# Block sums of W_down and of the stored middle tiles formed earlier and kept in device memory, in a fused transformer layer

## What is computed

```python
        hf = rms_norm(x, ffn_norm[l])
        gate_f, up = jnp.split(hf @ w_gate_up[l], 2, axis=-1)
        x = x + (jax.nn.silu(gate_f) * up) @ w_down[l]
```

## Time and profile before

| | us |
|---|---|
| median of 3 runs (1418.54 to 1420.36) | 1419.81 |
| the profiled execution | 1418.84 |
| its span on the core | 1416.9 |
| TensorE busy | 1297.3 (92%) |
| VectorE busy | 828.2 (58%) |
| ScalarE busy | 458.7 (32%) |
| GpSimd busy | 387.6 (27%) |

### The profile page before, as it was taken

The page is one execution under the profiler, slowest core; times in us unless marked ns, Lnnn a source line. Parts: engine busy times, 40 slices in busy tenths (PEclk is TensorE's granted clock), DMA queues, the critical chain, the costliest instruction groups (busy, mean ns, idle before and its releaser), DMA issues.

```text
span 1416.9 us, 16898 instructions
## 1 busy us (share of the span) xinstructions
PE 1297.3 (92%) x6028; PEld 1024.0 (72%) x6028; DVE 828.2 (58%) x1290; ACT 458.7 (32%) x758; POOL 387.6 (27%) x347
## 2 busy tenths in 40 slices
PE   4999999998898898999969999999999976898888
PEld 3688778886787777644448888888888855676777
DVE  5346778546455565313445555555555567887974
ACT  4221333341233322222343333333333333342421
POOL 3001101330121121100542333222333335564631
PEclk7899999998899999999979999999999998999999
DMA  6311334535521130031312222222224252414132
GB/s 205 107 46 30 107 87 132 169 134 139 182 71 57 45 91 9 0 132 61 104 30 90 87 69 84 74 90 90 90 89 157 67 187 74 134 45 145 36 99 85
DMA packets 155026, 132.00 MB, mean 93 GB/s; under 512 B 16638, under 2 KB 130636, under 8 KB 154956
## 3 DMA queue, kind: packets, MB, share of 16 engines
q1 hardware_dynamic: 154832, 131.03, 29.8%
q10 hardware_dynamic: 124, 0.04, 0.0%
HBM read 93.30 MB, written 36.70 MB: 92 GB/s over the span
## 4 chain that ended last, share of the span: by engine, by line
PE 71%; DVE 14%; issue 7%; ACT 4%; POOL 2%; DMA 2%; ACTq 0%; SPq 0%; DVEq 0%; POOLq 0%; PEldq 0%
PE ps L2028 28%; PE ps L1696 11%; PE ps L2033 9%; PE ps L1944 8%; PE ps L1820 5%; PE ps L1893 3%; DVE wop_lo L1597 2%; DVE dop_lo L1603 2%; DVE x L1658 2%; PE ps L1921 2%; PE ps L1909 1%; DMA w_pair<-hidden 1%; DVE stage L1346 1%; DVE row_stat L1549 1%; POOL mla_sc L777 1%
## 5 line engine op out<-in xcount | busy, mean ns | idle before, releaser
L2028 PE MATMUL ps<-xop_hi,wop_hi 128*128 128x512 f32 x616 | 242.3, 393 | 18.6 <-DVE wop_lo L1597 7.0
L2028 PE MATMUL ps<-xop_lo,wop_hi 128*128 128x512 f32 x616 | 241.6, 392 | 0.0
L2028 PE MATMUL ps<-xop_hi,wop_lo 128*128 128x512 f32 x616 | 241.4, 392 | 0.0
L2033 PE MATMUL ps<-dop_hi,wop_hi 128*128 128x512 f32 x308 | 126.9, 412 | 40.9 <-DVE x L1658 40.8
L1597 DVE TENSOR_TENSOR wop_lo<-w_sumS,wop_hi 128x512 fp32r<-128x512 f32 (+2 forms) x152 | 117.4, 773 | 79.5 <-ACT wop_hi L1117 79.5
L2028 PEld LDWEIGHTS ps<-xop_hi,wop_hi 128*128 128x128 f32 x616 | 116.8, 190 | 45.3 <-DVE wop_lo L1597 14.9
L2028 PEld LDWEIGHTS ps<-xop_hi,wop_lo 128*128 128x128 f32 x616 | 116.8, 190 | 24.5
L2028 PEld LDWEIGHTS ps<-xop_lo,wop_hi 128*128 128x128 f32 x616 | 116.8, 190 | 24.0
L856 POOL TENSOR_TENSOR w_sumS<-w_pair 128x512 f32<-128x512 f32 (+2 forms) x38 | 49.2, 1294 | 308.1 <-DVE wop_lo L1597 275.9
L1597 DVE TENSOR_TENSOR wop_lo<-w_pair,wop_hi 128x512 fp32r<-128x512 f32 (+2 forms) x114 | 101.3, 888 | 54.7 <-ACT wop_hi L1117 54.7
L1117 ACT ACTIVATE wop_hi<-w_sumS 128x512 fp32r<-128x512 f32 (+2 forms) x152 | 86.5, 570 | 124.2 <-PE ps L2033 66.4
(11 more groups left out here) (271 smaller groups left out, 2150.9 us busy)
## 6 DMA issues: line engine op xcount, KB each, us to landing
w_pair<-in_w_gate_up SPq DMA_DIRECT2D x44, 512.0 KB, 5.0
hidden<-up SPq DMA_DIRECT2D x22, 512.0 KB, 2.6
raw<-in_w_in SPq DMA_DIRECT2D x21, 512.0 KB, 4.4
wd_raw<-in_w_down SPq DMA_DIRECT2D x12, 768.0 KB, 10.3
w_pair<-hidden SPq DMA_DIRECT2D x24, 384.0 KB, 4.1
qkv_kept<-qkv_st SPq DMA_DIRECT2D x12, 512.0 KB, 5.3
qkvf<-qkv_kept SPq DMA_DIRECT2D x8, 768.0 KB, 5.0
raw<-in_x SPq DMA_DIRECT2D x8, 512.0 KB, 4.7
```

What stands on the lines that cost most here:

```text
L2028: last = pe.matmul(ps[:, bank, :], w[:, k, :], a[:, k, :], start=(p in ("P1", "P2", "P7") and k == 0 and w is wop_hi[s] and a is hi), stop ...
L2033: last = pe.matmul(ps[:, bank, :], w[:, k, :], a[:, k, :], start=(p in ("P1", "P2", "P7") and k == 0 and w is wop_hi[s] and a is hi), stop ...
```

## The change

`DOWN_GROUPS` goes from 4, 6, 6, 6 to 6, 6, 6, 4. Four sums of blocks of W_down are made for pairs of row tiles (`down_sums(jj)`, 11 times) by GpSimd during gate and up and kept in device memory (`down_sums`); the T operands of a group are then seven loads (`load_down(gi, j)`) and no sums. Of the middle tiles of groups 1 to 3 the four sums S1 to S4 are made in the same way, 8 times, once the second tile of a pair exists (`hidden_sums(jj)`), and kept (`hidden_sums`); a unit n >= 26 (`N_SPLIT`) is then seven loads of pieces (`d_pair`) and no sums. P2, P7 and P4 take two pairs of PSUM tiles in turn, so that P2 and P7 of unit n wait for unit n-2. The split of the T operands of the first down group starts after (21,P1), as before, and is spread over `DOWN_AFTER`. x comes back in halves.

```diff
 SMALL = 2 * GDN_HEADS + ROPE
 RAW, SPLIT = 4, 2
 BASE = 32
...
+        PIECES = 7
+        N_SPLIT = N_GATE + TT // 2
+        PAIR_TILES = [(sum(DOWN_GROUPS[:gi]) + j, sum(DOWN_GROUPS[:gi]) + kg // 2 + j)
+                      for gi, kg in enumerate(DOWN_GROUPS) for j in range(kg // 2)]
+        S_PAIRS = PAIR_TILES[DOWN_GROUPS[0] // 2:]
+        SECOND = {b: i for i, (a, b) in enumerate(S_PAIRS)}
+        WD_AT = {n: jj for jj, n in enumerate([n for n in range(N_GATE) if n not in SECOND][:len(PAIR_TILES)])}
...
+        DOWN_AFTER = {(N_GATE - 1, "P1"): (0, 0), (N_GATE - 1, "P2"): (0, 1), (N_GATE - 1, "P6"): (0, 2), (N_GATE, "P1"): (0, 3),
+                      (N_GATE - 1, "P3"): (0, 4), (N_GATE - 1, "P4"): (0, 5), (N_GATE, "P2"): (0, 6)}
+        for gi in range(1, len(DOWN_GROUPS)):
+            for j, p in enumerate(PRODUCTS):
+                DOWN_AFTER[N_GATE + gi * TT // 2 - 1, p] = (gi, j)
...
             def load_hidden(n):
...
                 sp.wait_ge(wop_ready, AT[n - 2, "P4"] + 1)
                 sp.wait_ge(hid_stored, 16 * (j0 + kg))
...
+                if gi == 0:
...
+                sp.wait_ge(hid_sums_kept, 3 * 16 * (i0 + kh))
+                if gi == 1 and row < 2:
+                    sp.wait_ge(dop_ready, 7)
+                    sp.wait_ge(hid_stored, 16 * HID_TILES)
...
+                to = d_pair[gi][n % 2]
...
+                                    ("A22", hid_d[j0 + kh:j0 + kg, :, high])):
+                    sp.dma_start(to[name][:, :, :], from_.rearrange("j p n -> p j n")).then_inc(wp_loaded[n % 2], 16)
...
+            def load_previous(jj):
+                if jj >= 1:
+                    sp.wait_ge(hid_sums_kept, 3 * 16 * jj)
+                sp.wait_ge(hid_stored, 16 * (S_PAIRS[jj][0] + 1))
...
+                sp.dma_start(hid_prev[:, :], hid_d[S_PAIRS[jj][0], :, :]).then_inc(prev_loaded, 16)
+
+            def keep_hidden_sums(jj):
+                sp.wait_ge(hid_sums, 4 * jj + 1)
+                sp.dma_start(hs_d[2, jj, :, :], hid_sum[0][:, :]).then_inc(hid_sums_kept, 16)
+                sp.wait_ge(hid_sums, 4 * jj + 3)
...
+                             hid_prev[:, :].rearrange("p (s n) -> p s n", s=2)).then_inc(hid_sums_kept, 16)
+                sp.wait_ge(hid_sums, 4 * jj + 4)
+                sp.dma_start(hs_d[3, jj, :, :], hid_sum[1][:, :]).then_inc(hid_sums_kept, 16)
...
+            def load_down_rows(jj):
+                if jj == 0:
...
+                    sp.wait_ge(gate0_silu, 2)
+                    sp.wait_ge(hid0_ready, 2)
+                else:
+                    sp.wait_ge(wd_sums_kept, 4 * 16 * jj)
+                for row, tile in enumerate(PAIR_TILES[jj]):
+                    sp.dma_start(wd_rows[row][:, :], w_down[0, tile * P:(tile + 1) * P, :]).then_inc(rows_ready, 16)
...
+            def keep_down_sums(jj):
+                sp.wait_ge(wd_sums, 4 * (jj + 1))
+                for k, part in enumerate((wd_rows[0][:, 0:BANK], wd_sum[:, :], wd_rows[0][:, BANK:], wd_rows[1][:, 0:BANK])):
+                    sp.dma_start(wt_d[k, jj, :, :], part).then_inc(wd_sums_kept, 16)
...
+            def load_down(gi, j):
...
+                if gi == 0 and j == 0:
...
+                if gi == 0 and j >= 3:
+                    sp.wait_ge(dop_ready, j - 2)
+                if gi >= 1:
+                    g = 7 * (gi - 1) + j
+                    sp.wait_ge(dop_ready, 7 + g - 3 if g >= 4 else 7)
...
-                                     "(j p) n -> p j n", p=P)).then_inc(wd_loaded, 16)
+                    k = ("P6", "P7", "P5", "P4").index(name)
+                    from_ = wt_d[k, jj:jj + kh, :, :].rearrange("j p n -> p j n")
+                sp.dma_start(wd_raw[gi][j][:, :, :], from_).then_inc(wd_loaded[raw_slot(gi, j)], 16)
...
             for n in range(N_GATE):
                 if n + 2 < N_GATE:
                     load_gate_up(n + 2)
...
+                if n in SECOND and n < N_GATE - 1:
+                    load_previous(SECOND[n])
+                if n - 1 in WD_AT:
+                    keep_down_sums(WD_AT[n - 1])
+                if n == N_GATE - 6:
+                    for j in range(3):
+                        load_down(0, j)
...
+                if n == N_GATE - 1:
+                    load_down(0, 6)
                 if n + 2 >= N_GATE:
                     load_hidden(n + 2)
+                keep_hidden(n)
+                if n == N_GATE - 2:
+                    load_down(0, 3)
+                if n in WD_AT:
+                    load_down_rows(WD_AT[n])
+                if n in SECOND and n < N_GATE - 1:
+                    keep_hidden_sums(SECOND[n])
+                if n == N_GATE - 2:
+                    load_down(0, 4)
+                    load_previous(SECOND[N_GATE - 1])
+                    load_down(0, 5)
...
+            for t in (1, 5, 2, 6, 3):
+                load_x2(t)
+            sp.wait_ge(hid1_ready, N_GATE)
+            load_x2(7)
+            keep_hidden_sums(SECOND[N_GATE - 1])
             for n in range(N_GATE, N_GATE + N_DOWN):
+                gi = group_of(n)
+                if row_of(n) == 3 and gi + 1 < len(DOWN_GROUPS):
+                    for j in range(4, 6):
+                        load_down(gi + 1, j)
                 if n + 2 < N_GATE + N_DOWN:
                     load_hidden(n + 2)
-                if row_of(n) == 0 and 1 <= group_of(n) < len(DOWN_GROUPS) - 1:
-                    load_down(group_of(n) + 1)
+                if n == N_GATE:
+                    for j in range(4):
+                        load_down(1, j)
+                if row_of(n) == 3 and gi + 1 < len(DOWN_GROUPS):
+                    load_down(gi + 1, 6)
+                    if gi + 2 < len(DOWN_GROUPS):
+                        for j in range(4):
+                            load_down(gi + 2, j)
...
+                n = S_PAIRS[jj][1]
+                a11, a21 = hid_prev[:, 0:BANK], hid_prev[:, BANK:]
+                pool.wait_ge(prev_loaded, 16 * (jj + 1))
...
+                pool.tensor_tensor(hid_sum[0][:, :], a11, a21, ALU.subtract).then_inc(hid_sums, 1)
+                pool.wait_ge(hid_sums, 4 * jj + 1)
+                pool.wait_ge(hid1_ready, n + 1)
+                pool.tensor_tensor(a21, a21, up[:, BANK:], ALU.add).then_inc(hid_sums, 1)
+                pool.wait_ge(hid_sums, 4 * jj + 2)
+                pool.tensor_tensor(a11, a21, a11, ALU.subtract).then_inc(hid_sums, 1)
+                pool.wait_ge(hid_sums, 4 * jj + 3)
+                pool.wait_ge(hid0_ready, n + 1)
+                pool.tensor_tensor(hid_sum[1][:, :], up[:, 0:BANK], a11, ALU.subtract).then_inc(hid_sums, 1)
+
+            def down_sums(jj):
+                b11, b12 = wd_rows[0][:, 0:BANK], wd_rows[0][:, BANK:]
...
+                pool.wait_ge(rows_ready, 2 * 16 * (jj + 1))
+                pool.tensor_tensor(wd_sum[:, :], b22, b12, ALU.subtract).then_inc(wd_sums, 1)
+                pool.wait_ge(wd_sums, 4 * jj + 1)
+                pool.tensor_tensor(b12, b12, b11, ALU.subtract).then_inc(wd_sums, 1)
+                pool.wait_ge(wd_sums, 4 * jj + 2)
+                pool.tensor_tensor(b11, wd_sum[:, :], b11, ALU.add).then_inc(wd_sums, 1)
...
+            for n in range(1, N_SPLIT):
+                if n - 2 in SECOND and n < N_GATE + 1:
+                    hidden_sums(SECOND[n - 2])
                 pair_sums(n)
-                if last_of is not None:
-                    down_sums_late(last_of)
+                if n == N_GATE + 1:
+                    hidden_sums(SECOND[N_GATE - 1])
+                if n - 2 in WD_AT:
+                    down_sums(WD_AT[n - 2])
...
-                if n >= N_GATE - 1 and (n - N_GATE + 1) % 4 == 0 and n < N_GATE + N_DOWN - 1:
+                if (n, p) in DOWN_AFTER:
                     act.wait_ge(product_done, q + 1)
-                    down_high((n - N_GATE + 1) // 4, PRODUCTS.index(p))
+                    down_high(*DOWN_AFTER[n, p])
 
...
                             dve.wait_ge(hid_stored, 16 * n)
+                        if n - 1 in SECOND:
+                            dve.wait_ge(hid_sums, 4 * (SECOND[n - 1] + 1))
                         dve.tensor_tensor(up[:, BANK:], snap4[:, :], c_bank, ALU.add).then_inc(up1_ready, 1)
...
                 elif p == "P2":
...
+                    if n < 2:
+                        pe.wait_ge(hT_ready, TT - 1 + n)
+                    elif n - 2 < N_GATE:
+                        pe.wait_ge(gate0_ready, n - 1)
                     else:
...
@@ -2020,7 +2152,7 @@
                         pe.wait_ge(snapped[{"P6": "P1", "P5": "P6", "P3": "P5"}[p]], n + 1)
                 else:
                     pe.wait_ge(added, DOWN_AT[n, {"P6": "P1", "P5": "P6", "P3": "P5", "P4": "P7"}[p]] + 1)
-                bank = {"P2": 4, "P7": 5, "P4": 5}.get(p, 2 + n % 2)
```

178 lines of the change are left out of this document (94 added, 84 removed).

## The result

The changed kernel takes 1384.8 us at the median of four runs (1381.9 to 1387.7) against 1420.1 (1418.5 to 1423.4) for the kernel before on the same chip: a ratio of 0.974, with a 95% interval of 0.972 to 0.976. The prediction was 1375, with a range of 1363 to 1395. The profiled execution took 1381.9 us, its span 1380.1. The four times lie in two pairs, near 1382 and near 1387.5, and the profile is of one of the lower pair.

The account below looks back on a forecast made before the run. The prediction saw gate and up at full pace and 61.0 us lost to TensorE waits and low clock at the seam, group changes and end. Recovering 47.8, 1418.84 - 47.8 - 1.9 + 5.5 = 1374.6, so 1375, range 1363 to 1395.

Parts of the forecast that it names:

- Start: At unit 1, P2 no longer waits for unit 0's `gate`, only for its own split: -1.9 us.
- Tile 2: Unit 3's loads queue behind the first W_down rows: 3.1 us waiting plus 2.4 low clock, +5.5.
- The other tiles: Remaining gate and up tiles: GpSimd's added sums are covered by VectorE's slack, tiles stay at 19.05 us, cost 0.
- rivals A: Gate and up: a `snap` or `up` comes late, 1 us in each of 19 tiles, 1394 us; chance 0.10.
- D: Gate and up: GpSimd and VectorE exclude each other, tiles reach 27.6 us, kernel slower than before; chance 0.04.
- Seam: Gate and up to down product: loss of 36.5 becomes about 6.7 us, 4.3 waiting for unit 23 plus 2.4 low clock.
- Changes of group: Down product: losses at the three changes become 2.0, 2.0 and 1.0 us, with GpSimd idle from unit 26.
- Rival E: Changes of group stay at 11.5 us each because VectorE, not GpSimd, holds them: 1404 us; chance 0.04.
- Units 26 to 37, the end: Down product: seven loads per unit narrowly hidden, 0; at the end, the 1.5 us loss stays.
- rival B: Down product loads come late, one wait at each of three changes, 25 us: 1400; chance 0.12.
- Low clock: TensorE after waits: 2.4 us charged for each wait of 3 us or more.
- Rival C: No new wait: unit 3 lands in time, or unit 23 before needed, or both: 1364 to 1370 us; chance 0.10.

Follow-up runs that it names:

- e1: Changed kernel with no rows of W_down in tile 0, their sums starting one tile later: 1378.0 us, ratio 0.970.
- e11: e1 plus four more GpSimd sums per tile in tiles 3 to 10, in gaps of its queue with nothing waiting for them: 1379.1 us, ratio 0.970.
- e7: e1 plus four more GpSimd sums in each of 11 tiles, the first W_down sum made five times: 1400.8 us, ratio 0.986.
- e2: Changed kernel with unit 23's loads issued ahead of the first down group's last T operand: 1382.3 us, ratio 0.973.
- e4: Changed kernel with the edits of e1, e2 and e3 together: 1369.3 us, ratio 0.964.
- e5: e4 with the first down group's last two T splits moved to after (22,P6) and (22,P5): 1370.3 us, ratio 0.964.
- e3: Changed kernel with each group's last T operand loaded ahead of the next unit's seven pieces: 1376.3 us, ratio 0.969.
- e8: Changed kernel without kept sums of middle tiles, units 26 to 37 being two loads and GpSimd's sums: 1382.5 us, ratio 0.973.
- e10: e5 with unit 24's loads ahead of four rows of x, and without kept sums of middle tiles: 1369.5 us, ratio 0.964.

## Why the prediction was right, and by how much it was off

The sign, the range and the likeliest mechanism were right: from the start of the block the change gave 36.1 us, forecast 44.2, and by the medians 35.3 where 45 were forecast. Two terms were mis-sized. Term by term, with losses counted as in the prediction (time less 0.2268 per matmul):

- **Start.** Forecast -1.9; measured 19.59 instead of 21.48 us to P2 of unit 1, -1.9. It was the split that it then waited for.
- **Tile 2.** Forecast 3.1 of waiting and 2.4 of low clock. The load landed at 771.2, P5 started at 773.1: 4.5 with the start of a product, and 1.2 of low clock (the starts of the 1668 matmuls span 379.3 us for 378.1). The sum, 5.7 for 5.5, was better than its parts; e1 confirms the mechanism.
- **The other tiles.** 0, as forecast, and rivals A and D fell with it. VectorE was busy 11.4 us per tile in e1 (22.7 in two), against 10.64 before and a bound of 15.0. The reason given, cover on VectorE, holds (e11) but was incomplete: the tighter limit is the ring of loads, sums and stores through SyncE's queue, whose turn e7 made longer than a tile. The prediction never worked it out.
- **Seam.** Forecast 4.3 + 2.4 = 6.7; measured 6.4 + 3.0 (the starts of 189 matmuls span 45.6 us for 42.6), 9.3. The order of events was the forecast's. Its mis-sized term is the load of unit 23: 5.5 us from the first issue to landing in the forecast, 7.9 here (1145.2 to 1153.05), with the transfer engines busy 0.9 of the stretch. e2, e4 and e5 add that VectorE's two T splits hold it by themselves, and e5 that the load of unit 24, thought hidden by 0.3 us, is the next.
- **Changes of group.** Forecast 2.0, 2.0 and 1.0; measured 4.4, 4.9 and 2.4. The mechanism for the first two waits was right to 0.3 us (0.4 and 1.4 forecast, 0.45 and 1.13 found). What failed is the sentence "followed through, ... the rest fits": I followed VectorE and left out SyncE, where seven issues of half a microsecond stand before the last T load. e3 shows it: that wait is 5.7 us in three changes, and without it they lose 2.4, 2.4 and 1.1, close to what the forecast had for VectorE alone. Rival E fell, with splits at 1.75 us.
- **Units 26 to 37, the end.** 0 and unchanged, as forecast; rival B fell.
- **Low clock.** The charge was 2.4 us for each wait of 3 us or more. What 50 matmuls behind a wait took beyond full pace was, at the seam, 3.0 us after a wait of 6.20, but 2.3 after 7.45 (e1), 1.7 after 5.70 (e8), and 2.6 and 1.7 after 4.68 and 4.69 (e2, e4); at tile 2 1.5 after 4.38; in e5 1.5 after 3.54. At the third waits it was 0.1 after 2.68 (changed kernel) and 2.77 (e11), but 1.7 after 2.43 (e11) and after 3.27 (e2). The length of a wait alone doesn't set its price: the charge was about right at the seam, too high at tile 2, and there is a price below 3 us in some executions.

The misses are 2.6 at the seam and 6.7 at the changes, 9.3, where the whole is 8.1. Most of the difference is luck: the 48 matmuls behind the start of (1,P2) lost 2.5 us to a short wait and low clock in this profile and 3.4 in the one before, 0.9 that nobody forecast (the runs have 2.5 to 3.9 there). Rival C fell with the two waits. Of the parts of the change, the kept sums of W_down and the order of the groups (not taken apart here) carry nearly all: e8 has them without the middle sums and is as fast. The kept middle sums, by themselves worth about 4 us in all (e10), were spent on the queue that their seven loads lengthen.

One reading of the prediction was too weak. The Trainium skill, "Trainium Architecture — The Big Picture", What this means for kernel authors, calls the ports of VectorE and GpSimd an exclusive lock, and the prediction found that the trace agrees in part. It agrees almost to the letter. In gate and up of the profile before (740 to 1130 us), 63 VectorE instructions with two SBUF inputs start while a GpSimd sum runs, and every one ends 0.54 to 0.56 us after that sum does, however long it had to stand. The same in e11:

```profile
855.90 1.29 POOL L986 TENSOR_TENSOR w_sumS<-w_sumS,w_pair 128x512 f32<-128x512 f32 x1
855.94 1.79 DVE L1792 TENSOR_TENSOR up<-up,gate 128x512 f32<-128x512 f32 x1
```

The sum ends at 857.19, the instruction at 857.73. So the 1.1 us by which such an instruction grows are not a price on top of the sums but the rest of a sum that is under way, and rival D's 27.6 us for a tile counted them twice. Alone the instruction takes 0.69 us, so each hand-over saves about 0.14 against the lengths in the records. That is how twelve GpSimd sums at 1.29 us and nine such instructions at 0.69, 21.7 us together, fit in e11 into a tile of 19.05 with nothing late.

## What to carry to other kernels

When a change moves work to an idle engine through memory, follow the queue that carries the data as closely as the engines: here the engines had room to spare, and what was lost was lost to the order of issues on one queue (5.7 us in tile 2, 5.7 at the changes, and, with the order on VectorE, most of the 9 at the seam). Work out the turn of each ring of load, compute, store and issue, and compare it with the period it must fit; that number, not busy time, says how much more work it takes. After taking a wait away look for what it covered, and count a gain only when the next wait is known.

## What the runs showed of the hardware

- A VectorE instruction with two SBUF inputs that starts while a GpSimd sum runs ends a fixed time after the sum: 0.54 to 0.56 us for 128x512 (63 of 63 before, where it takes 0.69 alone), 1.61 for a T split of 128x1536 (1.75 alone), so 4.44 behind a sum of blocks of 3.67. A sum behind a VectorE instruction grows likewise: 1.63 us for 1.29 in e7, 2.51 for 1.0 behind the T split that ends at 1274.50 before.
- A VectorE instruction with one PSUM input is not held: 42 of 128x512 that start 0.6 us or more before the end of a GpSimd sum in the profile before took 0.67 to 0.69 us.
- GpSimd busy 16.9 us of a 19.05 us tile, waits included, cost TensorE nothing and made VectorE 1.4 us busier per tile than in e1 (e11).
- Issues on SyncE's queue took 0.33 to 0.65 us each, so twelve were 6.6 to 7.75 us. T loads of 768 KB landed in 6.4 us at the median from `down_sums` and in 7.6 from W_down in the changed kernel.
- The same instructions ahead of the changed part took 701.4 to 707.7 us with different granted clocks, more than several of the effects that were looked for.
